# Five token buffers at the start, a re-sorted router and a weight ring whose second half waits for the first gather, in a hybrid decoder step on Trainium2

## What is computed

```python
h = x @ w_in                                   # 1024 -> 2320
# two mixers side by side: gated linear attention, and sliding-window attention with sinks
mix = concatenate([o_gla, o_swa]) @ w_out
x1 = layer_norm(ALPHA * x + mix, ln1_g, ln1_b)
logits = x1 @ w_router + b_router              # 32 experts
top_val, top_idx = top_k(logits, 4); gate_w = softmax(top_val)
# per expert e, on the tokens routed to it:
h = clamped_swiglu(xe @ w_gate[e] + b_gate[e], xe @ w_up[e] + b_up[e])
y = h @ w_down[e] + b_down[e]
ffn[token] += gate_w * y
x2 = layer_norm(ALPHA * x1 + ffn, ln2_g, ln2_b)
```

## Time and profile before

| what | value |
|---|---|
| time, median of 3 runs | 1460.9 us (1460.77 to 1462.64) |
| the profiled execution: its time | 1461.05 us |
| its span, first to last instruction | 1459.1 us |
| mean granted clock of PE | 0.976 |
| busy PE / DVE / ACT / POOL | 1393.9 / 468.0 / 325.3 / 115.3 us |
| chain that ended last: PE, DVE, ACT, DMA | 90%, 4%, 2%, 2% |
| moved by DMA | 463.93 MB, mean 318 GB/s |

### The profile page before, as it was taken

One profiled execution on the slowest core, in us unless ns is written; L12 is line 12 of the kernel. 1 busy time (PEld: TensorE's weight loads), 2 busy tenths in 40 slices (PEclk: granted clock), 3 DMA queues, 4 the chain that ended last, 5 costly groups with the idle time before them and its releaser, 6 DMA issues.

```text
span 1459.1 us, 37797 instructions
## 1 busy us (share of the span) xinstructions
PE 1393.9 (96%) x16616; PEld 946.7 (65%) x16616; DVE 468.0 (32%) x891; ACT 325.3 (22%) x668; POOL 115.3 (8%) x119
## 2 busy tenths in 40 slices
PE   6999999997999999999999999999999999999991
PEld 5777776555566666666666666666666666666660
DVE  3245556364422223222222222222222222222224
ACT  3544466121021111111111211111111111111114
POOL 1022000001001000000000010001000000100000
PEclk9999999996999999999999999999999999999996
DMA  7211032566999999999999999999999999999944
GB/s 246 89 49 44 15 120 92 210 235 261 362 402 395 396 387 396 398 396 388 398 400 398 397 399 397 389 396 400 397 386 399 398 397 400 397 399 386 396 165 143
DMA packets 78468, 463.93 MB, mean 318 GB/s; under 512 B 12400, under 2 KB 13632, under 8 KB 29008
## 3 DMA queue, kind: packets, MB, share of 16 engines
q1 hardware_dynamic: 67616, 429.54, 73.9%
q0 software_dynamic: 10192, 31.31, 8.4%
q10 hardware_dynamic: 512, 0.79, 0.1%
HBM read 444.70 MB, written 22.22 MB: 320 GB/s over the span
## 4 chain that ended last, share of the span: by engine, by line
PE 90%; DVE 4%; ACT 2%; DMA 2%; issue 1%; DVEq 0%; POOL 0%; SPq 0%; ACTq 0%; POOLq 0%
PE unit L1248 42%; PE unit L1251 27%; PE unit L1157 4%; PE unit L1231 2%; PE unit L756 2%; PE unit L758 2%; PE unit L757 2%; PE unit L1236 2%; PE unit L751 1%; PE unit L1175 1%; DMA xbuf<-x_prompt_dram 1%; PE unit L908 1%; PE unit L884 1%; PE unit L791 1%; DVE attT L2175 1%
## 5 line engine op out<-in xcount | busy, mean ns | idle before, releaser
L1248 PE MATMUL unit<-ring_b,xeT 128*32 128x512 f32 (+1 forms) x3168 | 353.5, 488 | 1.1 <-ACT xeT L1411 1.1
L1251 PE MATMUL unit<-ring_b,xeT 128*32 128x256 f32 x1584 | 354.0, 381 | 0.0
L1251 PE MATMUL unit<-ring_a,xeT 128*32 128x256 f32 x1488 | 330.7, 379 | 0.0
L1248 PE MATMUL unit<-ring_a,xeT 128*32 128x256 f32 (+1 forms) x2976 | 330.2, 486 | 0.0
L1251 PEld LDWEIGHTS unit<-ring_b,xeT 128*32 128x32 f32 x1584 | 171.4, 110 | 56.3 <-issue 0.7
L1251 PEld LDWEIGHTS unit<-ring_a,xeT 128*32 128x32 f32 x1488 | 161.8, 110 | 52.5
L1251 PE MATMUL unit<-ring_a,heT 128*32 128x256 f32 x768 | 169.7, 379 | 0.0
L1248 PE MATMUL unit<-ring_a,heT 128*32 128x512 f32 (+1 forms) x1536 | 169.4, 486 | 0.0
L1248 PEld LDWEIGHTS unit<-ring_b,xeT 128*32 128x32 f32 x3168 | 126.5, 110 | 60.4 <-issue 4.3
L1251 PE MATMUL unit<-ring_b,heT 128*32 128x256 f32 x720 | 160.3, 379 | 0.0
L1248 PE MATMUL unit<-ring_b,heT 128*32 128x256 f32 (+1 forms) x1440 | 160.1, 486 | 0.0
(11 more groups left out here) (322 smaller groups left out, 1601.5 us busy)
## 6 DMA issues: line engine op xcount, KB each, us to landing
ring_b<-w_gate_dram SPq DMA_DIRECT2D x68, 1024.0 KB
ring_a<-w_down_dram SPq DMA_DIRECT2D x68, 1024.0 KB
ring_b<-w_up_dram SPq DMA_DIRECT2D x64, 1024.0 KB
ring_a<-w_up_dram SPq DMA_DIRECT2D x64, 1024.0 KB
ring_a<-w_gate_dram SPq DMA_DIRECT2D x60, 1024.0 KB
ring_b<-w_down_dram SPq DMA_DIRECT2D x60, 1024.0 KB
raw_a<-w_in_dram SPq DMA_DIRECT2D x16, 512.0 KB, 3.6
xbuf<-x_prompt_dram SPq DMA_DIRECT2D x4, 512.0 KB, 5.4
```

The lines of the kernel that those rows point to most:

```text
L1248: return mm(out[j * NS:(j + 1) * NS, a:b], stat(j), w[:, a:b], start=first, stop=last)
L1251: return mm(out[CAP:P, j * 256:(j + 1) * 256], stat(j), w[:, FOLD:D], start=start, stop=stop)
```

## The change

1. All five token tiles are loaded at the start, one after the other, behind `ck` and ahead of all weights: tiles 0 and 1 into `xbuf`, tiles 2 to 4 into a new `xlate` that lies over `qk` and `gv`, which are written later. Each has its own semaphore. `ce` is loaded after chunk 4 instead of chunk 1, and POOL waits for tile 4.
2. The router is re-sorted. On PE: transposes of tile 4 ahead of logits 2, logits 4 ahead of the transposes of tile 3, and 13 filler matmuls (`keep_running`, lines 1053 to 1057: 32 x 256 columns, never read) in front of five steps. On ACT: `x1_in(2)` ahead of `std(3)`, and a one-off exponential of a scratch tile ahead of `x1_in(3)`. On DVE: `route` ends at the masks, the gates become `gate(i)`, and `gate(4)` and `gate(3)` follow `route(3)`; `top8` and `ntop` get two buffers. On POOL: the gates are stored tile by tile in five DMAs, each when its tile is ready.
3. Ring slots 8 to 15 all wait for tile 3's output product, all norms and the landing of gather 0 (`x_rows`).
4. Some semaphores are merged (`selo`, `ones_ready`, `xb_ready`).

```diff
-TAIL = [... "x1T2", "logit2", "x1T4", "x1T3", "logit4", "logit3"]
+TAIL = [... "x1T2", "x1T4", "logit2", "logit4", "x1T3", "logit3"]
@@
+        here[0] = qk_at
+        xlate = sb("xlate", [P, NT - 2, D])
@@
+        def x_rows_in(i):
+            return xbuf[:rows(i), i] if i < 2 else xlate[:rows(i), i - 2]
@@ SP
-            for i in range(2):
-                sp.dma_start(xbuf[:rows(i), i], d["x_prompt"][0, i * P:(i + 1) * P]).then_inc(x_in[i], 16)
+            for i in range(NT):
+                src = d["x_prompt"][0, i * P:(i + 1) * P] if i < PT else d["x_sample"].rearrange("n t d -> (n t) d")
+                sp.dma_start(x_rows_in(i), src).then_inc(x_in[i], 16)
@@
-                if n == 1:
+                if n == R1 - 1:
                     sp.dma_start(ce[:], d["early"][:, :]).then_inc(const_in, 16)
-                if 1 <= n <= 3:
-                    i = n + 1
-                    sp.wait_ge(*filled(f"x{i - 2}"))
-                    src = ...
-                    sp.dma_start(xbuf[:rows(i), i % 2], src).then_inc(x_in[i % 2], 16)
@@
                     if m == 8:
                         sp.wait_ge(*filled("out3"))
-                    if m == 14:
                         sp.wait_ge(x1_ready, NT)
+                        sp.wait_ge(x_rows, 16)
@@ POOL
-            pool.wait_ge(x_in[0], 32)
+            pool.wait_ge(x_in[PT], 16)
@@
-            pool.wait_ge(gates_ready, NT)
-            pool.dma_start(x1_dram[0:SEQ, D:XCOLS].rearrange("(i p) e -> p i e", p=P), gd[:, 0:PT]).then_inc(x1_out, 16)
-            pool.dma_start(x1_dram[SEQ:T, D:XCOLS], gd[:NS, PT]).then_inc(x1_out, 16)
-            pool.wait_ge(x1_out, 16 * (NT + 2))
+            for n, i in enumerate(TILES):
+                pool.wait_ge(gates_ready, n + 1)
+                pool.dma_start(x1_dram[i * P:i * P + rows(i), D:XCOLS], gd[:rows(i), i]).then_inc(x1_out, 16)
+            pool.wait_ge(x1_out, 16 * 2 * NT)
@@ PE
             x1_transposes(2)
+            x1_transposes(4)
+            keep_running("logit2", 2)
             logits(2)
-            x1_transposes(4)
+            keep_running("logit4", 2)
+            logits(4)
+            keep_running("x1T3", 2)
             x1_transposes(3)
-            logits(4)
+            keep_running("logit3", 3)
             logits(3)
+            keep_running("pos", 4)
@@ ACT
+            x1_in(2)
             std(3)
-            x1_in(2)
             x1_in(4)
+            st(nc.scalar.activation(snm[:], srr[:], ACT.Exp, scale=0.0))
+            x1_in(3)
             gate_exp(2)
-            x1_in(3)
             gate_exp(4)
             gate_exp(3)
@@ DVE
                 v.sem_inc(mask_ready, 1)
+
+            def gate(i):
+                n, r = TILES.index(i), rows(i)
                 v.wait_ge(g_exp, n + 1)
@@
             route(0)
+            gate(0)
             first_norm(4)
             route(1)
+            gate(1)
             first_norm(3)
             route(2)
             route(4)
+            gate(2)
             st(cp(row_part[:, 3:4], k_("slot")[:, 3:4]))
             route(3)
+            gate(4)
+            gate(3)
```

More of the change, by code:

```diff
@@ L416, in build @@
             "down_bias_in", "gate_bias_in", "up_bias_in", "gdT_ready"))
-        x_in = [sem(f"x_in{n}") for n in range(2)]
+        x_in = [sem(f"x_in{n}") for n in range(NT)]
+        def x_rows_in(i):
+            return xbuf[:rows(i), i] if i < 2 else xlate[:rows(i), i - 2]
         raw1_in = [sem(f"raw1_in{n}") for n in range(R1)]
@@ L445, in build @@
             "picked", "tok_done", "idx_ready", "x_rows", "xT_done", "xe_ready"))
-        gate_read, sig2, h_ready, queries_ready, ones_ready = (sem(n) for n in (
-            "gate_read", "sig2", "h_ready", "queries_ready", "ones_ready"))
+        gate_read, sig2, h_ready, queries_ready = (sem(n) for n in (
+            "gate_read", "sig2", "h_ready", "queries_ready"))
         h_part, hT_done, he_ready, y_part, y_ready, y_stored = (sem(n) for n in (
@@ L761, in _ @@
             for i in range(NT):
-                pe.wait_ge(x_in[i % 2], 16 * (i // 2 + 1))
-                transposes(f"x{i}", lambda k, i=i: xbuf[:rows(i), i % 2, k * P:(k + 1) * P], i)
+                pe.wait_ge(x_in[i], 16)
+                transposes(f"x{i}", lambda k, i=i: x_rows_in(i)[:, k * P:(k + 1) * P], i)
             def weights_product(g, piece=None):
@@ L1593, in sample_out @@
                 act.wait_ge(*has("sel"))
-                st(copy(qkv[:NS, PT, 0:512], side("sel")[:NS, 0:512]), selo)
-                act.wait_ge(selo, 1)
+                st(copy(qkv[:NS, PT, 0:512], side("sel")[:NS, 0:512]), sample_act)
+                act.wait_ge(sample_act, 3)
                 act.sem_inc(s_room("sel"), 1)
@@ L1749, in gate_exp @@
                 r = rows(i)
-                st(nc.scalar.activation(gate4[:r, i], top8[:r, 0:TOPK], ACT.Exp, bias=ntop[:r]), g_exp)
+                par = TILES.index(i) % 2
+                st(nc.scalar.activation(gate4[:r, i], top8s[:r, par, 0:TOPK], ACT.Exp, bias=ntops[:r, par:par + 1]), g_exp)
             mix_in(0)
@@ L2261, in _ @@
             st.settle()
-            v.wait_ge(x_in[0], 64)
+            v.wait_ge(x_in[0], 32)
             v.wait_ge(ln_in, 96)
@@ L2293, in route @@
                 v.sem_inc(s_freed(name), 1)
-                if n:
-                    v.wait_ge(g_exp, n)
+                top8, ntop = top8s[:, n % 2], ntops[:, n % 2:n % 2 + 1]
+                if n > 1:
+                    v.wait_ge(g_exp, n - 1)
                 st(nc.vector.max(top8[:r], lg[:r]))
@@ L2369, in _ @@
             st.settle()
-            v.sem_inc(xb_ready, 1)
+            v.sem_inc(mask_ready, 1)
             v.wait_ge(tok_done, 1)
```

25 lines of the change are left out of this document (12 added, 13 removed).

## The result

The kernel after takes **1448.88 us** (median of 4 runs, 1446.61 to 1449.42) against 1460.84 (1458.61 to 1462.64): ratio 0.9914, 95% interval 0.9900 to 0.9929. The forecast was 1450.5 in a range of 1446.4 to 1457.4. The profiled execution has a span of 1445.9 (1459.1 before), a time of 1448.46 and a mean clock of 0.983 (0.976).

The account below looks back on a forecast made before the run. The loop was taken as bound by the tensor engine with DMA nearly saturated, start and router by dependency chains. From 1461.05, -6.0 (start), -7.0 (router) and +2.5 (ring and end) gave 1450.5 us, range 1446.4 to 1457.4.

Parts of the forecast that it names:

- The start: Start, up to the first product: tokens loaded ahead of weights bring it earlier by 6.0 us, ends -4.5 and -6.4.
- The router: Router stage: new order, fillers and tile-wise gate stores land the first gather 7.0 us earlier, bounds -5.1 and -8.2.
- The ring: Expert loop: eight weight loads held until the gather use up the lead; with the late scatter-add +2.5 us.
- The slack is gone, and the last chunk waits about 1 us: End of the expert loop: 13.5 us of slack in the weight loads vanishes; weights end +1076 after the gather.
- PE waits for weights before the last two experts: Expert loop: named as a sign that the forecast is wrong; 0 to 3 us of waits were expected in the last experts.
- a scatter-add that is not late: End of the kernel: named as a sign that the forecast is wrong; it was expected 2.8 us late at most.
- Rival 1: Expert loop: the slowest engine takes 2.87 to 2.88 us a load, 6 us more, 1453 to 1458; chance 18%.
- the second, slower end: Expert loop: loads slow further, gain used up at 2.895 us a load, 1470 us at 2.917; chance 5%.
- the scatter-add of the last but one expert: End of the kernel: weights still flowing make it land at 1430.2, 2.8 us late at most.
- the three terms: Whole kernel: start -6.0, router -7.0, and ring with the end effect +2.5 us.

Follow-up runs that it names:

- experiment 1: Kernel before with only the new start (five token buffers, constants later, POOL waiting for tile 4), against the kernel before: 1454.55 us against 1461.92, ratio 0.9945.
- experiment 5: The kernel after, unchanged, run and profiled once more on the chip of the next three kernels: 1452.41 us, ratio 0.9938 to the kernel before.
- experiment 7: Kernel after, but only ring slots 12 to 15 wait for the gather; 8 to 11 load after tile 3's output product: 1447.86 us, ratio 0.9909.
- experiment 9: Kernel after, with ring slots 8 to 15 also waiting until PE has used the first weight slot: 1455.5 us, ratio 0.9956.

## Why the prediction was right

**The start: right in kind, its size somewhat too large.** Forecast -6.0, ends -4.5 and -6.4; the pair measured -5.35, and the eleven profiles with the new start have the first product between 15.50 and 16.92 (mean 16.35), the whole span of "15.0 or 16.9". The transposes ended at 12.10, between the forecast's 11.0 and 12.9, since tiles 2 to 4 took 3.38 and not the "1.04 us each if the clock is up"; the 3.90 us behind them are the 4.0 of the forecast. That the gain passes whole is shown by experiment 1.

**The router: right almost to the step.** Counted from tile 2's transposes, forecast and measured are: logits 3 done 10.2 and 10.9, masks complete 13.4 and 13.2, positions taken up 16.0 and 15.8, row numbers 18.6 and 18.4, gather landed 24.3 and 23.6, first product 27.0 and 26.69. The store landed in 1.7 instead of 2.2, which changed nothing, since row numbers bind. The gather took 4.2 instead of 4.77, but less than half of the 0.7 us that it was early reached the first product: PE's down biases, which the forecast left out, ended 0.5 us after it. The term of -7.0 measured -7.28. "Fillers are 13 matmuls of some 0.2 us each" was wrong: each is two passes, 26 in all at 0.22 to 0.24. It did no harm because they stand in waits; logits 2 alone start 0.36 later than without them (+2.56, +2.20).

**The ring: the mechanism right, its place too late, its end effect wrong.** "The slack is gone, and the last chunk waits about 1 us": the b2 gap fell from 13.2 to 3.4 and PE waits 1.0 us (2.1 in the second profile), but at 1319 and 1348, in the down products of the fourth and third last experts, and not at the last chunk. The last wait is 66 us ahead of PE's end, and in the second profile the first is already at 1253. The forecast had named "PE waits for weights before the last two experts" and a scatter-add that is not late as signs of being wrong, and both came, while `b2` landed 0.8 us before the last chunk began and not after. The reading of when the lead ends was therefore wrong; its size was not.

Weights were done 1407.9 - 334.1 = 1073.8 after the gather, forecast +1076. In all kernels in which eight slots wait for the gather, the b2 gap is 3.2 to 3.5 whatever else differs, and in all others 9.6 to 13.5: the load stream and not PE's own pace seems to set that gap. That is the strongest sign that this is a debt and not a chance wait.

A part of the +1.87 is something else: expert 1's transposes come 15.23 after expert 0's instead of 14.78. PE does not wait for the second gather there; its clock rises from 0.50 to 1.00 some 4.4 us after expert 0's first product instead of 3.5, and products at half the clock for 0.9 us longer make the 0.45. Waits of 1.0 and this are 1.46; the last 0.4 are not accounted for. Rival 1 asked for 2.87 to 2.88 us a load; 2.845 to 2.856 came, so it fell, and the second, slower end with it.

The step of the sum that failed is "the scatter-add of the last but one expert ... now weights still flow: 1430.2, 2.8 late at most". It landed in 5.3, and the tail is the same:

```profile
L695 POOL DMA_INDIRECT acc_rows<-ysb,idx x1: 1447/1447/1447, 1407.3 to 1407.3; - x1
...
DMA to landing us min/median/max: 5.3/5.3/5.3
```

```profile
1400.00:1404.00 4.00, 4.00 (x59) 2.48 (x55) 0.00 (x0) 0.10 (x1) 0.00 (x0) 1.00 0.19 76
1404.00:1408.00 4.00, 4.00 (x62) 2.64 (x58) 0.00 (x0) 2.44 (x5) 0.65 (x1) 1.00 0.15 65
```

A share of 0.15 of sixteen engines is 2.4 engines' work: most of them have nothing left when the scatter-add is issued. And the weights were done at 1407.9, only 0.6 us after its issue, where the forecast (+1076 against 1073.8) let them flow longer. It finished at 1412.6 at no loss. Loop and tail together cost +1.8 where the forecast had +2.5.

**The middle: a gain that was not forecast.** -2.38 us came from a stage that the change does not touch; with it the three terms overshoot (-5.35, -7.28, +1.8 give -10.8, the span fell 13.2). The forecast of 1450.5 is 2 us above 1448.46 for this reason. The medians differ by 12.0 us in the first comparison and by 10.4 in the second (experiment 5), on both sides of the 10.8 of the three terms. How much of the 2.38 is luck of the profiled pair and how much the new start brings is open, as the last section shows.

The rule of the Trainium skill (DMA: Bandwidth & Descriptors, Rules for kernel authors) to issue early and wait late was the ground for the first rival. Here both of its sides are measured: issuing all eight loads early costs 2.80 us at the gather, issuing all eight late costs 1.1 to 2.7 in the loop, and four of each costs neither. The statement of the Trainium skill (DMA: Bandwidth & Descriptors, Latency and other measured facts) that two engines are usually slower fits the 2.4 engines' work above; the share is a mean over all engines, so no row here shows which ones lag or why.

## What to carry to other kernels

A prefetch that competes with a small DMA on the critical path is better split than moved: here only the loads still in flight when the small one goes out had to wait (experiment 7). At a DMA share of 1.00 the stream won back only a part of the lead that it was denied (experiment 9). Read the lead from the landing of the last load behind the stream against the end of the loop. Fillers pay where they end inside a wait; price one from its passes in the trace before choosing how many, since ten where five fit gave back all they won.

## What was not expected of the hardware

**The clock falls in the middle in some executions and not in others.** The same pause is followed by a fall in one execution and not in another. One-us windows (columns as in the earlier trace rows), first of the kernel without fillers, then of the kernel after, second profile; this stage is the same code in both:

```profile
161.00:162.00 1.00, 0.00 (x0) 0.00 (x0) 0.62 (x3) 0.96 (x4) 0.00 (x0) 0.88 0.00 0
162.00:163.00 1.00, 0.59 (x3) 0.62 (x4) 0.42 (x1) 0.81 (x3) 0.00 (x0) 0.50 0.00 0
```

```profile
161.00:162.00 1.00, 0.05 (x1) 0.00 (x0) 0.65 (x4) 0.88 (x4) 0.00 (x0) 1.00 0.00 0
162.00:163.00 1.00, 0.50 (x5) 0.53 (x6) 0.42 (x1) 0.81 (x3) 0.00 (x0) 1.00 0.00 0
```

PE is idle for 0.7 and then 1.45 us in both; in the first the granted clock drops from 1.00 to 0.50 (2.4 to 1.2 GHz) for 6.8 us, in the second it stays at 1.00. Such falls, there, at 220 to 232 and at 49 to 58 (PE busy throughout that one), make the middle 294.5 to 300.1 us. The spread of the runs goes with them: ten executions of the kernel after have spans of 1444.1 to 1448.3 at a mean clock of 0.982 to 0.984 in seven cases, and 1451.5 to 1452.4 at 0.979 to 0.980 in three. All three profiles of kernels with the old start show a fall within 165 to 174, and three of eleven with the new one (at 161 to 169). So the new start may also make the falls rarer, which would be the rival of experiment 1; fourteen profiles don't decide it. With fillers in the two pauses the spreads of two kernels were 4.1 and 3.4 us, against 5.1 to 9.9 in the other kernels with the new start (2.8 in the four executions of the first comparison), and neither profile shows a fall there. That points to the pauses as a source but does not show it: the fall at 49 to 58 has no pause. The Trainium skill (TensorE: Matmul & The Clock Gate, What's actually happening) says of a kernel's first matmuls that the number at the lower clock differs from run to run; here the falls in the middle differ from run to run too. The middle alone differs by up to 5.6 us between profiles, so single profiles are compared stage by stage.

**SyncE's issues get long well before PE waits.** In the loop of the kernel before single issues took over 0.5 us only from 1250 on; after, from about 650 on, up to 8.1 us (median about 2). PE's first wait for a weight comes at 1319 (at 1253 in the second profile), 600 us and more after the first long issue. That a queue is full is the likely reason, but no view shows the queue's depth.
